# Small tiles in front of h, and large tiles at multiples of 2048 bytes in each partition

## What is computed

```python
h = rms_norm(x, norm_mix_pre)
proj = einsum("btd,dp->btp", h, w_in) + b_in             # 2048 -> 11272 columns
y_a = hgrn2_mix(...)                                     # 8 heads of 128, chunks of 64, recurrent state
y_b = mlstm_mix(...)                                     # 4 heads, 128 x 256 state
merged = sigmoid(gate_a) * (y_a @ w_up_a) + sigmoid(gate_b) * (y_b @ w_up_b)
x = x + rms_norm(merged @ w_out, norm_mix_post)
h = rms_norm(x, norm_ffn_pre)
gate = causal_dwconv(h @ ffn_w_gate, ffn_conv_w, ffn_conv_b)   # width 3
x = x + rms_norm((gelu(gate) * (h @ ffn_w_up)) @ ffn_w_down, norm_ffn_post)   # d_ff = 5632
```

## The kernel before

| tile | bytes | begins at | by 2048 | by 64 |
|---|---|---|---|---|
| h_hi, h_lo | 32768 each | 16512, 49280 | 128 | 0 |
| raw, w_hi, w_lo | 16384 each | 82048, 98432, 114816 | 128 | 0 |
| prm | 1536 | 131200 | 128 | 0 |
| ident | 512 | 132736 | 1664 | 0 |
| small | 1056 | 133248 | 128 | 0 |
| arena | 94720 | 134304 | 1184 | 32 |
| m_prev | 20 | 229024 | 1696 | 32 |

## Time and profile before

### The profile page before, as it was taken

The page is one execution under the profiler, slowest core; times in us unless marked ns, Lnnn a source line. Parts: engine busy times, 40 slices in busy tenths (PEclk is TensorE's granted clock), DMA queues, the critical chain, the costliest instruction groups (busy, mean ns, idle before and its releaser), DMA issues.

```text
span 2946.1 us, 32534 instructions
## 1 busy us (share of the span) xinstructions
PE 2903.5 (99%) x13167; PEld 2398.1 (81%) x13167; DVE 1150.0 (39%) x1141; ACT 823.0 (28%) x741; POOL 87.9 (3%) x99
## 2 busy tenths in 40 slices
PE   7999999999999999999999999999999999999997
PEld 6888888888888888888888888888888888888886
DVE  4232334244333333432644343443433343343436
ACT  3243434332222222222431222222222222122224
POOL 1000001000000000000000000000000000000003
PEclk9999999999999999999999999999999999999999
DMA  4334333433333334334433233333333333333334
GB/s 181 88 88 110 88 88 98 111 94 94 91 90 93 89 100 157 128 129 171 142 87 100 87 99 100 90 95 100 97 88 100 100 85 100 100 95 90 100 95 162
DMA packets 402657, 309.16 MB, mean 105 GB/s; under 512 B 5662, under 2 KB 349858, under 8 KB 401072
## 3 DMA queue, kind: packets, MB, share of 16 engines
q1 hardware_dynamic: 393824, 283.13, 32.7%
q0 software_dynamic: 4176, 16.95, 1.7%
q10 hardware_dynamic: 4608, 8.39, 0.8%
HBM read 295.87 MB, written 12.58 MB: 105 GB/s over the span
## 4 chain that ended last, share of the span: by engine, by line
PE 95%; DVE 2%; ACT 1%; POOL 1%; issue 0%; DMA 0%; DVEq 0%; SPq 0%; ACTq 0%
PE ps L653 21%; PE ps L382 18%; PE ps L656 11%; PE ps L385 9%; PE ps L401 7%; PE ps L403 7%; PE ps L402 7%; PE ps L599 6%; PE ps L673 1%; PE ps L675 1%; PE ps L674 1%; DVE w_lo L1122 1%; ACT w_hi L703 0%; DVE arena L1143 0%; PE ps L619 0%; PE ps L518 0%
## 5 line engine op out<-in xcount | busy, mean ns | idle before, releaser
L1122 DVE TENSOR_TENSOR w_lo<-raw,w_hi 128x2048 fp32r<-128x2048 f32 x260 | 597.6, 2298 | 1031.2 <-ACT w_hi L703 1031.2
L703 ACT CAST w_hi<-raw 128x2048 fp32r<-128x2048 f32 x260 | 496.1, 1908 | 632.3 <-PE ps L403 490.1
L656 PE MATMUL ps<-h_hi,w_lo 128*128 128x512 f32 x1376 | 325.9, 389 | 0.0
L653 PE MATMUL ps<-h_hi,w_hi 128*128 128x512 f32 x1376 | 325.9, 389 | 0.0
L653 PE MATMUL ps<-h_lo,w_hi 128*128 128x512 f32 x1376 | 325.9, 389 | 0.0
L653 PEld LDWEIGHTS ps<-h_hi,w_hi 128*128 128x128 f32 x1376 | 258.2, 188 | 53.7
L656 PEld LDWEIGHTS ps<-h_hi,w_lo 128*128 128x128 f32 x1376 | 258.3, 188 | 53.6
L653 PEld LDWEIGHTS ps<-h_lo,w_hi 128*128 128x128 f32 x1376 | 258.3, 188 | 53.6
L382 PE MATMUL ps<-h_hi,w_hi 128*128 128x512 f32 x1152 | 279.5, 395 | 1.1 <-ACT w_hi L703 1.1
L385 PE MATMUL ps<-h_hi,w_lo 128*128 128x512 f32 x1152 | 272.9, 389 | 0.0
L382 PE MATMUL ps<-h_lo,w_hi 128*128 128x512 f32 x1152 | 272.8, 389 | 0.0
(11 more groups left out here) (259 smaller groups left out, 2477.0 us busy)
## 6 DMA issues: line engine op xcount, KB each, us to landing
raw<-in_w_in SPq DMA_DIRECT2D x88, 1024.0 KB, 5.6
raw<-in_ffn_w_down SPq DMA_DIRECT2D x48, 1024.0 KB, 5.0
raw<-in_ffn_w_gate SPq DMA_DIRECT2D x44, 1024.0 KB, 5.6
raw<-in_ffn_w_up SPq DMA_DIRECT2D x44, 1024.0 KB, 5.6
raw<-in_w_out SPq DMA_DIRECT2D x20, 1024.0 KB, 5.0
merge_gates<-arena ACTq DMA_DIRECT2D x32, 256.0 KB, 2.0
raw<-in_w_up_a SPq DMA_DIRECT2D x8, 1024.0 KB, 5.3
raw<-in_w_up_b SPq DMA_DIRECT2D x8, 1024.0 KB, 5.3
```

Source lines behind the costliest of these rows:

```text
L653: pe.matmul(ps[:, bank + s, :], w[0][:, j, :], k[:, j, :], start=(k is h_hi and j == 0), stop=False)
L656: mm = pe.matmul(ps[:, bank + s, :], w[1][:, j, :], h_hi[:, j, :], start=False, stop=(j == KT - 1))
L703: act.copy(w_hi[:, s, :], raw[:, s, :]).then_inc(hi_ready, 1)
L1122: dve.tensor_tensor(w_lo[:, s, :], raw[:, s, :], f32(w_hi[:, s, :]), ALU.subtract).then_inc(lo_ready, 1)
```

## The change

`small`, `m_prev` and `ident` are allocated first. Then a filler, `to_line`, takes the bytes up to the next multiple of 2048 (`LINE`). After it come `h_hi`, `h_lo`, `raw`, `w_hi`, `w_lo` and the arena, all of whose sizes up to the arena are multiples of 2048, so each of them begins at a multiple of 2048. `prm` goes behind the arena and is cut from 384 to 344 columns, of which the kernel writes and reads no more than 344. Worked out by the rule of 32 bytes: small 16512, m_prev 17568, ident 17600, filler of 320 bytes from 18112, h_hi 18432, h_lo 51200, raw 83968, w_hi 100352, w_lo 116736, arena 133120, prm 227840 to 229216. No instruction is added, taken away or moved in its order.

```diff
+LINE = 2048
@@
+        small = sb("small", [P, 264])
+        m_prev = sb("m_prev", [ML_H, TT + 1])
+        ident = sb("ident", [P, P])
+        here = nc.sbuf_base
+        sb("to_line", [P, (-here % LINE) // 4])
+        assert nc.sbuf_base % LINE == 0
         h_hi = sb("h_hi", [P, KT, T], F32R)
         h_lo = sb("h_lo", [P, KT, T], F32R)
         raw = sb("raw", [P, RING, U])
         w_hi = sb("w_hi", [P, RING, U], F32R)
         w_lo = sb("w_lo", [P, RING, U], F32R)
-        prm = sb("prm", [P, 384])
-        ident = sb("ident", [P, P])
-        small = sb("small", [P, 264])
@@
         ctx.enter_context(nc.sbuf_tensor("arena_keep", [P, ARENA], F32))
+        prm = sb("prm", [P, 344])
@@
-        m_prev = sb("m_prev", [ML_H, TT + 1])
```

## The result

The kernel after takes 2930.40 us (median of 4 runs, 2929.47 to 2931.23), beside 2947.82 us for the kernel before: ratio 0.994, 95% interval 0.9928 to 0.9952. That is 17.4 us less, 0.6%. The forecast was 2927.2 us with a range of 2918 to 2949. The time was met. The mechanism given for it was not what the experiments show.

A forecast was written before the change was run, and what follows sets the result against it. TensorE was taken as the bound, matmul count times distance. Arena alignment 19.5 us plus small matmuls 1.0 gave 20.5 off the 2946.1 us span, 2925.6; with 1.6 carried over, 2927.2 us, range 2918 to 2949.

The forecast's parts named there:

- The bound: Whole span: TensorE busy 99%, 95% of the chain; time is the number of matmuls times their distance.
- the weight feed: TensorE's waits: the feed of weights was said to cost it about a microsecond.
- Which matmuls would change, and to what: Down products 14.1 us, lifting 5.1, L518 0.3: 6.67 ns less per matmul, 19.5 us in all; h with weights unchanged.
- One 64-byte piece more per matmul: Arena operands off a multiple of 64: rows straddle 33 pieces in place of 32, costing 6.67 ns a matmul.
- The same price in both roles: Arena operands: slower by the same 6.67 ns whether moving (ya, yb) or stationary (act, wg).
- Crossing a line of 2048: Moving h rows: crossing costs nothing, as both groups of 16 in L619 take 2.08 us.
- The float32 matmuls: Recurrences and transposes with operands in the arena: gain of 0 to 5.4 us, taken as 1 us.
- Head, tail and long units: Head and tail put at 0, within 1 us; two long cm units more or less give 3.6 us scatter.
- No change: Arena operands are slow because of region, not alignment; time stays at 2947.7 us, give or take 2; chance 0.10.
- Rival 2: Matmuls with h and weights lose their 13.3 ns surplus too: 2765 us, or 2846 for half; chance 0.13.
- Rival 3: Down products: stationary act and moving weights at equal low address bits collide, 2955 or 2970 us; chance 0.05.
- The Trainium skill: SBUF cachelines of 16 bytes: a multiple of 32 is already aligned, so the time would stay at 2947.7 us.

The follow-up runs named there:

- arena64: Kernel before with small at 272 columns in place of 264, arena 32 bytes later at a multiple of 64: 2944.53 us, ratio 0.9989 to before.
- all32: Kernel after with the filler 32 bytes longer, so h, weight slots and arena begin 32 bytes past a multiple of 2048: 2930.35 us, ratio 0.9939.
- arena256: Kernel before with small widened to 320 columns, arena 224 bytes later, h and weights unmoved: 2930.82 us, ratio 0.9941.
- half_cols: Kernel after with half the stationary columns (128 x 64) in the gate and up products, half their computation left out: 2941.74 us, one run.
- mixed64: Kernel after without the filler, with gaps putting h_hi, h_lo, weight slots and arena at different multiples of 64: 2977.45 us, ratio 1.0101 to before.
- hi32: Kernel after with h_hi and w_hi 32 bytes past a multiple of 64, h_lo, w_lo and arena at multiples of 64: 3003.67 us, ratio 1.019.
- sw2: Kernel after, no filler, h_hi, h_lo, w_hi, w_lo and arena at 248, 252, 0, 24 and 32 by 256: 3001.45 us, one run.
- sw1: Kernel after, no filler, h_lo, w_hi, w_lo and arena 240, 256, 336 and 352 bytes past h_hi's remainder by 512: 2979.44 us, one run.

## Why the prediction was right in its time and wrong in its reason

*The bound.* Right: TensorE, as the number of matmuls times the distance of their starts. The account above closes to 0.2 us with such distances and three stretches that scatter from execution to execution. One reading was off without effect: the weight feed does not cost TensorE about a microsecond but some 4, since the waits on `w_lo` come on top (L401 behind L1122, 2.9 us before and 3.0 after).

*Which matmuls would change, and to what.* Right: 2112 + 768 + 48, from 233.3 to 226.7 ns, 19.5 us. Cm units unchanged, as said.

*Why.* Wrong. The step that failed reads "One 64-byte piece more per matmul, because the row straddles 33 pieces in place of 32, is just the difference seen". arena64 removed the straddling and kept 233.3 ns in the down products and L518; all32 made every row straddle and kept 226.7 everywhere. The cost follows the distance in bytes between the moving and the stationary start: at a multiple of 256 it is absent, at all others tried it is 1.4 to 7.1 ns a matmul within groups of one pair. Before, the table of addresses had two differences between fast and slow kinds, 32 by 64 for the arena alone and 1056 between the arena and the weights, and the prediction took the first because 64 bytes pass in 6.67 ns. That match was a coincidence, as far as the runs bear out; what the table's other values lie over 226.7 (2.3 ns at 229.0, 5.6 at 232.3) is no multiple of 6.67.

That the time was met is luck in one respect. The forecast took the fast kinds' measured 226.7 ns for the arena too, and the change put all starts at a multiple of 64 and all distances at a multiple of 2048 at once, so that either reason gives this figure. For arena64 the same reason gave 2927 to 2933 us, and 2944.53 was measured.

*The same price in both roles*, which the prediction noted in passing, was a hint: what belongs to one row need not cost the same for a streamed row and for a stationary tile a quarter as long. But the price of a pair need not be the same in both roles either. It was so before, at +32 and -32; in arena64, at +64 and -64, it is 228.9 and 233.3 ns.

*Crossing a line of 2048.* Right that it costs nothing: all32 makes every moving row of 512 columns cross one, where after has none that does, and both have 226.7 ns.

*The float32 matmuls.* 1 us was taken, nothing came: the group of 16 that took 1.79 us takes 1.78 after, and the other groups with float32 operands in the arena took the same time in both traces to 0.02 us, but for the transposes of L428 (0.14 us less of 38). This term is the one mis-sized, within its bounds.

```profile
306.85 1.78 PE ps L489 x16
```

*Head, tail and long units.* 3.6 us of scatter were allowed; one long unit more, the longer L623 and the quicker head together make up 2.3 us. The forecast of 2927.2 missed by 3.2 us through these and the 1 us above. L623's stretch came behind the transposes of the second norm and a wait of TensorE; the windows of after show PE busy for 1.76 of 3.50 us, and then a granted clock of 0.65:

```profile
1481.00:1484.50 3.50, 1.76 (x13) 1.16 (x12) 3.44 (x6) 2.29 (x4) 0.00 (x0) 1.00 0.00 0
1484.50:1488.00 3.50, 3.42 (x20) 3.45 (x21) 0.00 (x0) 0.00 (x0) 0.00 (x0) 0.65 0.02 5
```

L619 shows no such stretch before, with the same wait ahead of it. It is no matter of the layout: arena256, in which h and the weights lie as before, has the long form (13.32 us), and half_cols, with the layout of after, the short one (11.75 us). Why it comes and goes is open.

*The rivals.* No change: refuted, and with it the region (arena64 and arena256 move the arena by 32 and 224 bytes and get a fifth and the whole of the gain). Rival 2, h and the weights gain as well: did not come, and all32 takes the ground from its skip to a border of 256; that the figure of 256 turns up again, now as the period of the distance, is as near as it came. Rival 3 had the sign of its mechanism reversed: equal low bits do not collide, they are the fast case, as its own counter-argument had noted of h and the weights. A layout that spreads the tiles, which rival 3 would favour, costs 47 us (mixed64 against after).

The Trainium skill, "SBUF — State Buffer", Specifications (TRN2), gives lines of 16 bytes. The prediction put beside it that by this rule the change would bring nothing. It did bring 17 us, but through a relation between two operands that this rule does not speak of; and since -4 and -8 bytes of distance cost 3 and 7 ns, the runs show no grain of 16 bytes in it.

*What stays open.* Why a distance that is a multiple of 256 is the fast one, what the remaining 13.3 ns are, why the sign counts, and why the clock falls behind the short matmuls. That the effect sits in TensorE's own two reads is argued and not tested by itself. For it speak the pair in hi32 (ya_hi with w_hi and with w_lo, in one stage) and that a distance has the same price to a few tenths of a nanosecond in stages in which VectorE and ScalarE do quite different work (+64 in mixed64 and arena64).

## What to carry to other kernels

Where fp32r matmuls of 512 columns stand back to back, let the moving and the stationary operand begin at a distance that is a multiple of 256 bytes in the partition, for all pairs that take turns: it was worth 3% of such a matmul, and small tiles inserted in the wrong places can cost it unseen (hi32, 2.5% of the whole kernel). Absolute alignment bought nothing here, so a wider small tile does what a filler to a line does. When a number fits a mechanism as well as 6.67 ns fitted a 64-byte piece, look in the same table for a second difference between the fast and the slow rows, and make the run that changes the one and keeps the other.

## What was not expected of the hardware

- The distance in bytes between the two operands of a matmul sets 226.7 to 233.8 ns between fp32r matmuls of 512 columns in groups of one pair, and -4 bytes already costs 3.1 ns.
- The sign of that distance counts: -64 has 233.3 ns, +64 has 228.9; -16 has 233.1, +16 has 228.1.
- Where three pairs take turns, one at distance 0 in three did not help (233.3 ns in hi32), and three at small distances had 235.6 (sw2).
- The slower rhythm is carried on for about eight matmuls into a group whose own distance is a multiple of 256 (sw1).
- Halving the columns of the stationary operand made the matmuls slower, 229.8 for 226.7 ns, although the loads took 134 for 188 ns.
- The granted clock of a stretch behind short float32 matmuls was 0.56 with TensorE busy all the while. Such a stretch came in two or three of four alike iterations, and not in the same ones when the program was run again.
